# A retrieval layer's expert values: 160 instead of 128 tokens by gathered rows, 416-column matmuls, and a quarter of the value splits on GpSimd

## The reference, cut to what matters

```
eidx = ...        # per token: 8 heads x 16 experts out of 16384
gate = softmax(best_s)
u = u_tab[ib];  a = einsum('bd,bhkd->bhk', hb, u)
a = gelu(a) * gb
return einsum('bhk,bhkd->bd', a, v_tab[ib])     # 128 value rows of 2048 numbers per token
```

## Time and profile before

| | us |
|---|---|
| runs (three) | 5164.22, 5155.04, 5153.08; median 5155.04 |
| the profiled execution's own time | 5158.61 |
| its span, first to last instruction | 5157.0 |
| TensorE busy (x34141 matmuls) | 5036.2 (98%) |
| VectorE busy | 2321.4 (45%) |
| ScalarE busy | 1301.7 (25%) |
| GpSimd busy | 1060.5 (21%) |
| mean granted TensorE clock | 0.987 |

### The profile page before, as it was taken

The page is one execution under the profiler, slowest core; times in us unless marked ns, Lnnn a source line. Parts: engine busy times, 40 slices in busy tenths (PEclk is TensorE's granted clock), DMA queues, the critical chain, the costliest instruction groups (busy, mean ns, idle before and its releaser), DMA issues.

```text
span 5157.0 us, 86673 instructions
## 1 busy us (share of the span) xinstructions
PE 5036.2 (98%) x34141; PEld 4840.3 (94%) x34141; DVE 2321.4 (45%) x4396; ACT 1301.7 (25%) x1709; POOL 1060.5 (21%) x800
## 2 busy tenths in 40 slices
PE   8999999999998999999999999999999999999897
PEld 7999999999997999999999999999999999999797
DVE  4333442234326796122222200002788888888633
ACT  3113332133212112222222222222222222222232
POOL 1000000110000034333333344443212222212000
PEclk9999999899999999999999999999999999999998
DMA  5553345455543443345444443334777777777322
GB/s 171 156 159 114 122 154 161 135 161 169 168 122 97 147 139 104 106 159 179 159 163 163 159 157 104 104 133 166 262 258 255 274 261 258 266 260 249 106 74 77
DMA packets 503983, 855.15 MB, mean 166 GB/s; under 512 B 32496, under 2 KB 368384, under 8 KB 485008
## 3 DMA queue, kind: packets, MB, share of 16 engines
q1 hardware_dynamic: 188224, 472.44, 27.8%
q0 software_dynamic: 45296, 246.67, 12.7%
q10 hardware_dynamic: 270336, 134.25, 9.3%
HBM read 766.86 MB, written 222.56 MB: 192 GB/s over the span
## 4 chain that ended last, share of the span: by engine, by line
PE 95%; DVE 2%; issue 1%; ACT 0%; DMA 0%; DVEq 0%; ACTq 0%; POOL 0%; POOLq 0%
PE PS L1566 64%; PE PS L2016 24%; PE PS L1989 2%; PE PS L1590 1%; DVE h_lo L960 1%; PE PS L1680 0%; PE PS L1935 0%; PE PS L1618 0%; PE PS L1706 0%; PE PS L1823 0%; DVE rstd L936 0%; DVE hf L954 0%; PE PS L1813 0%; PE PS L1694 0%; ACT w_hi L589 0%
## 5 line engine op out<-in xcount | busy, mean ns | idle before, releaser
L1566 PE MATMUL PS<-h_hi,w_hi 128*128 128x288 f32 x7808 | 1715.0, 301 | 52.3 <-DVE h_lo L960 42.4
L1566 PE MATMUL PS<-h_hi,w_lo 128*128 128x288 f32 x7808 | 1680.1, 297 | 0.0
L1566 PE MATMUL PS<-h_lo,w_hi 128*128 128x288 f32 x7808 | 1678.3, 297 | 0.0
L1566 PEld LDWEIGHTS PS<-h_hi,w_hi 128*128 128x128 f32 x7808 | 1262.4, 190 | 93.5 <-issue 63.5
L1566 PEld LDWEIGHTS PS<-h_hi,w_lo 128*128 128x128 f32 x7808 | 1264.7, 190 | 0.0
L1566 PEld LDWEIGHTS PS<-h_lo,w_hi 128*128 128x128 f32 x7808 | 1264.4, 190 | 0.0
L589 ACT ACTIVATE w_hi<-w_raw 128x1024 fp32r<-128x1024 f32 x522 | 553.6, 1061 | 2307.3 <-PE PS L1566 2274.3
L519 POOL TENSOR_TENSOR w_lo<-w_raw,w_hi 128x1024 fp32r<-128x1024 f32 x254 | 618.9, 2437 | 1530.5 <-ACT w_hi L589 1530.5
L925 DVE TENSOR_TENSOR w_lo<-w_raw,w_hi 128x1024 fp32r<-128x1024 f32 x270 | 330.1, 1224 | 661.4 <-ACT w_hi L589 646.0
L1481 DVE TENSOR_TENSOR x<-x,PS 128x448 f32<-128x448 f32 x512 | 307.6, 618 | 229.0 <-PE PS L2016 220.9
L1418 DVE TENSOR_SCALAR oh_j<-iota,oh_cur 128x128 f32<-128x128 f32 x448 | 126.4, 282 | 585.0 <-PE PS L1989 584.9
(11 more groups left out here) (276 smaller groups left out, 4794.9 us busy)
## 6 DMA issues: line engine op xcount, KB each, us to landing
w_raw<-in_w SPq DMA_DIRECT2D x652, 512.0 KB, 4.1
v_rows<-in_w ACTq DMA_DIRECT2D x512, 256.0 KB, 3.7
v_raw<-in_w SPq DMA_DIRECT2D x128, 512.0 KB, 5.2
act_scr<-gsp POOLq DMA_DIRECT2D x128, 288.0 KB, 3.8
gate_scr<-g_st POOLq DMA_DIRECT2D x14, 2048.0 KB, 9.0
gl<-act_scr SPq DMA_DIRECT2D x32, 896.0 KB, 4.9
g_in<-gate_scr SPq DMA_DIRECT2D x32, 896.0 KB, 9.4
spill_scr<-spill POOLq DMA_DIRECT2D x40, 288.0 KB, 4.8
```

The source lines that it names most:

```text
L1566: ins = mm(dst[:, a], w[:, m, at + n], xx[:, k, a * TH:(a + 1) * TH], start=first and n == 0 and r == 0, stop=last and n == len(ks) - 1 an ...
```

## The change

- TG goes from 128 to 160 = P + TX tokens, TD from 448 to 416, ND from 14 to 13. The 32 extra tokens lie on four partitions each: partition 32q+t has experts 32q to 32q+31 of token 416+t. So each of the 32 groups now has GR_X = 5 rows, four for the 128 tokens and one (i = 4) for the extra ones, added to an accumulator of its own, `acc_x`; 160 rows, picks and `axpy` in all, five row buffers.
- `axpy` also runs in group 0 (at j = 3 to 7); in the others at j = 1, 2, 3, 6, 7, in the last at 0, 1, 2, 4, 5.
- The low part of the blocks with b % 4 == 2 is made on GpSimd (`value_low` there, semaphore `v_lop`), which has it in one order with `row` and `pick`; who waited for `v_lo` of such a block waits for `v_lop`.
- At the end 16 matmuls of 32 columns against `sel_x` sum the four partitions of each extra token; one more addition to x; TensorE waits for the additions before the next projection.
- The gate stage has 13 blocks of 32 tokens, the last outside the loop. Buffers are laid out anew.

```
-TG = 128
+TX = 32
+TG = P + TX
+GR_X = 5
+NK_G = GR_X * TX
...
+        def lowered(b):
+            q = b % 4
+            return ("v_lop", b // 4 + 1, 2) if q == 2 else ("v_lo", 3 * (b // 4) + min(q, 2) + 1, 6)
... (SyncE)
-                    sp.wait_ge(S["v_lo"], at_step(b - 3, bl))
+                    name, n, per = lowered(b - 4)
+                    sp.wait_ge(S[name], at_step(n, [(r, per * c) for r, c in loops]))
                     value_load(b, loops)
... (GpSimd)
+            def row(n):
+                if n >= GR_X:
+                    pool.wait_ge(S["axpy"], n - GR_X + 3)
+                pool.indirect_dma_start(rows[:, n % GR_X], None, v_rows, ...
+            def value_low(b):
+                pool.wait_ge(S["v_hi"], b + 1)
+                q = v_slot(b)
+                nc.gpsimd.tensor_tensor(q[2], q[0], q[1].bitcast(F32), ALU.subtract).then_inc(S["v_lop"], 1)
             pool.wait_ge(S["index"], 1)
             for u in range(2):
                 pool.wait_ge(S[f"asp{u}"], 16 * (PRE // 2))
             pool.wait_ge(s_used, B_PG)
+            pool.wait_ge(S["v_hi"], 3)
+            value_low(2)
             nc.gpsimd.memset(acc[:], 0.0).then_inc(S["axpy"], 1)
-            pick(0, 8)
+            nc.gpsimd.memset(acc_x[:], 0.0).then_inc(S["axpy"], 1)
+            for n in range(2 * GR_X):
+                pick(n)
             pool.wait_ge(S["relaid"], 32 * NV)
-            for k in range(P):
-                row(k)
-                if k % 8 >= 4 and k < P - 8:
-                    pick(8 * (k // 8 + 1) + 2 * (k % 4), 2)
+            for n in range(GR_X):
+                row(n)
+            for g in range(NG):
+                for i in range(GR_X):
+                    if g < NG - 1:
+                        row(GR_X * (g + 1) + i)
+                    if g < NG - 2:
+                        pick(GR_X * (g + 2) + i)
+                    if i == 1:
+                        value_low(8 * g + 6)
+                    if i == 3 and g < NG - 1:
+                        value_low(8 * g + 10)
... (VectorE, the indices)
-            ch.did(v.tensor_tensor(f_sel[:], iota[:], ident[:], ALU.mult))
+            quarters = [slice(TX * q, TX * q + TX) for q in range(4)]
+            src_x = slice(TD % P, TD % P + TX)
+            ch.did(v.tensor_tensor(f_one[:], iota[:], ident[:], ALU.mult))
+            ch.did(v.tensor_reduce(sel_x[:], ident[:].rearrange("p (e t) -> p t e", e=4), AX.X, ALU.add))
+            for r in quarters:
+                ch.did(v.tensor_copy(g_sel[r, :, 4], gij[src_x, TD // P, 0, r]))
...
+            for r in quarters:
+                ch.did(v.tensor_scalar(tok_x[r], part[r], float(TD - r.start), None, ALU.add))
+                ch.did(v.scalar_tensor_tensor(f_sel[r, :, 4], gij[src_x, TD // P, 1, r], float(NK),
+                                              gij[src_x, TD // P, 2, r], ALU.mult, ALU.add))
...
+            ch.did(v.tensor_scalar(f_sel[:, :, 4], f_sel[:, :, 4], float(T), tok_x[:], ALU.mult, ALU.add))
... (VectorE, the value stage)
+                turns = (0, 1, 2, 4, 5) if not more else (3, 4, 5, 6, 7) if g == 0 else (1, 2, 3, 6, 7)
                 if g:
                     dve.wait_ge(S["v_free"], at_step(KD * g, fl))
+                if turns[0] < 3:
+                    picked(g, loops)
                 for j in range(8):
...
-                    if more or j < 5:
+                    if (more or j < 5) and (j + 3) % 4 != 2:
                         value_low(8 * g + j + 3, loops)
...
+                    if j == 3 == turns[0]:
+                        picked(g, loops)
+                    if j in turns:
+                        axpy(g, turns.index(j), loops)
... (TensorE)
-            pe.wait_ge(S["axpy"], P + 1)
+            pe.wait_ge(S["axpy"], NK_G + 2)
...
+            for f in range(KD):
+                ins = mm(PS[:, 0, f * TX:(f + 1) * TX], acc_x[:, f * P:(f + 1) * P], sel_x[:], start=True, stop=True)
+            ins.then_inc(S["gx_t"], 1)
+            pe.wait_ge(S["gx"], 9)
```

More of the change, by code:

```diff
@@ L545, in _ @@
                     pool.dma_start(d["g_scr"][i * 2 + u], g_st[:, u]).then_inc(S[f"gput{u}"], 16)
+            for c in range(4):
+                put(UA + UG - 4 + c)
+            pool.wait_ge(S["g_ev"], 8 * ND + 2)
+            pool.dma_start(d["g_scr"][ND - 1], g_st[:, 0]).then_inc(S["gput0"], 16)
             puts(UA + UG, NCHUNK - 2 - UA - UG)
@@ L548, in _, with pick @@
             put(NCHUNK - 1, more=False)
[L551 to L564, removed]
+            def pick(n):
+                pool.indirect_dma_start(a_el[:, n:n + 1], None, act_flat,
+                                        bass.IndirectOffsetOnAxis(ap=act_i[:, n // GR_X, n % GR_X].unsqueeze(1), axis=0)
+                                        ).then_inc(S[f"el{n // GR_X % 2}"], 16)
+            def row(n):
+                if n >= GR_X:
+                    pool.wait_ge(S["axpy"], n - GR_X + 3)
+                pool.indirect_dma_start(rows[:, n % GR_X], None, v_rows,
+                                        bass.IndirectOffsetOnAxis(ap=row_i[:, n // GR_X, n % GR_X].unsqueeze(1), axis=0)
+                                        ).then_inc(S[f"row{n % GR_X}"], 16)
+            def value_low(b):
+                pool.wait_ge(S["v_hi"], b + 1)
+                q = v_slot(b)
+                nc.gpsimd.tensor_tensor(q[2], q[0], q[1].bitcast(F32), ALU.subtract).then_inc(S["v_lop"], 1)
             pool.wait_ge(S["index"], 1)
@@ L838, in _ @@
                         relay(i * 4 + (2 * s + c // 2), 6 + c % 2)
-            late = [(n, j) for n in range(4 * (ND // 2 - 1), N_FEAT) for j in (6, 7)]
+            for c in range(4):
+                beside(ND - 1, c)
+                relay(4 * (ND // 2 - 1) + c // 2, 6 + c % 2)
+            late = [(n, j) for n in range(4 * (ND // 2 - 1) + 2, N_FEAT) for j in (6, 7)]
             for c, (n, j) in enumerate(late):
@@ new lines, in axpy @@
+            def axpy(g, i, loops=()):
+                dve.wait_ge(S[f"row{i}"], at_step(16 * (g + 1), loops, 16))
+                n = GR_X * g + i
+                kl = [(r, GR_X * c) for r, c in loops]
+                dve.wait_ge(S["axpy"], at_step(n + 2, kl))
+                dst = acc if i < 4 else acc_x
+                v.scalar_tensor_tensor(dst[:], rows[:, i], a_sel[:, bass.ds(at_step(n, kl), 1)], dst[:], ALU.mult,
+                                       ALU.add).then_inc(S["axpy"], 1)
@@ L1487, in values @@
                         product(GRP * (g + 1) + (j + 1) // 2, loops)
-                    if k0 is not None and (j % 2 == 1 or not more):
-                        axpy(k0 + (j // 2 if more else j), [r for r, n in loops])
+                    if j == 3 == turns[0]:
+                        picked(g, loops)
+                    if j in turns:
+                        axpy(g, turns.index(j), loops)
             for c in range(GRP):
@@ L1493, in _ @@
                 low(c)
-            for b in range(3):
+            for b in range(2):
                 value_low(b)
@@ L1497, in _ @@
             with dve.Fori(0, (NG - 2) // 2) as i:
-                picked(0, [i])
                 for g in range(2):
-                    values(1 + g, [(i, 2)], k0=4 * g)
-            picked(P // 8 - 1)
-            values(NG - 1, more=False, k0=P - 8)
+                    values(1 + g, [(i, 2)])
+            values(NG - 1, more=False)
             dve.wait_ge(S["v_free"], 2 * NV)
```

103 lines of the change are left out of this document (56 added, 47 removed).

## The result

The changed kernel takes **5096.95 us** (median of four runs, 5095.67 to 5102.61); the kernel before, on the same chip, 5159.63 us (four runs, 5153.08 to 5165.33). The ratio is 0.9881 with a 95% interval of 0.9864 to 0.9898: faster by about 63 us. The forecast was 5087 us, between 5066 and 5120.

A forecast was written before the change was run, and what follows sets the result against it. The value stage was taken as bound by TensorE's matmul stream. Terms -85.2 - 6.6 + 2.1 + 18.5 + 2.0 + 1.4 = -67.8 took the profiled 5158.6 to 5090.8, median 5087 us, range 5066 to 5120.

The forecast's parts named there:

- The matmuls: Value stage: 416 columns instead of 448 take each matmul from 202.7 to 188.8 ns, 85 us less.
- rival of a pace set by weight loads: Value matmuls: weight loads, not columns, set the pace, so little is gained; about 5150 us, 2%.
- The gate stage: Gates: one block of 32 tokens fewer, 4 chunks x 16 small matmul instructions, 6.6 us less.
- The index block: Before the first one-hots: 14 more small VectorE instructions at 0.15 us, 2 us more, between 1 and 4.
- VectorE in a group: Value stage group: VectorE's work sums to 30.8 us against 36.25 on TensorE, so by itself it fits.
- the splits on GpSimd: Value groups: each shuts VectorE out up to 2.39 us, 4.8 a group: 35.6 of 36.25 us.
- hand-made plan: One value group laid out by instruction: GpSimd's split from 22.55 to 24.95 us, block 6 with 2.2 us to spare.
- No stall in a running group: Value groups: TensorE never waits, cost 0; bounds 0 to 2 us a group if a split comes late.
- rival of small stalls: Value groups: GpSimd misses the additions' gap; 0.5 to 2 us in 31 groups, 5102 to 5150 us, 14%.
- The start of the stage: Value stage, group 0: GpSimd's queue delays row 0 and block 6; TensorE stalls 18.5 us, plus 2 at low clock.
- The end: After the value matmuls: 16 extra small matmuls and one addition cost 1.4 us more, between 0.5 and 3.5.
- Slower: Value groups: `row`, `pick`, `axpy`, split form a ring making VectorE the bound; needs 2.2 us stall a group; 5%.

The follow-up runs named there:

- e6: Changed kernel with VectorE's index block spread over the eight steps of the last gate block instead of ahead of the first one-hots; 5092.00 us.
- e2: Changed kernel with GpSimd's order at the value stage's start altered: clearings, block 2's split, five picks, five rows, block 6's split, other picks; 5087.81 us.
- e5: e1 with GpSimd clearing its accumulators before waiting for the activations, then five picks, rows 0 to 4, then group 1's picks; 5074.27 us.
- e9: e5 and e6 together, with group 0's five `axpy` at j = 2, 3, 5, 6, 7 instead of 3 to 7; 5072.03 us.
- e10: e5 and e6 together, with the loads of blocks 4 and 5 issued ahead of the last activations' wait and group 2's loads; 5063.74 us.
- e4: Kernel before the change with only the quarter of the splits moved to GpSimd; 5177.92 us, ratio 1.0015 to 1.0056.
- e1: Changed kernel with all 256 splits on VectorE again; 5080.09 us.

## Why the prediction was right

- **The matmuls.** The step from two paces to a third held: 188.8 ns forecast, 188.89 measured. The rival of a pace set by weight loads is out.
- **The gate stage** held to the tenth: -6.6.
- **The index block** was a little undersized: 0.15 us an instruction gave 2.1, and 2.9 was measured. The four copies took 0.85 us together where 0.6 was put. The larger thing was not asked: the block stood on the path before the change too, and e6 takes it off for 7.6 us.
- **VectorE in a group, and the splits on GpSimd.** That a GpSimd split costs VectorE up to 2.39 us was right (2.0 and 2.2 here), and so was VectorE's busy time, 34.7 us against at most 35.6. The step that failed is "it fits": the sum put VectorE's waits at nothing, and it waits 1.8 us a group, mostly behind ScalarE, so that its round takes 36.53 us and not less than TensorE's 36.27. In group 1 the hand-made plan still holds, but for the pick that takes 3.07 us and not 1.51 beside an `axpy`: the split begins at 23.3 us instead of 22.55. Then it slips by 0.26 us a group to 24.8, the 2.2 us to spare are gone, and it falls on VectorE's split and not on additions. "No stall in a running group" became 0.24 to 0.28 us in 16 groups and 4.4 with its low clock once, 9.6 us in all with smaller waits in a few others. That is less than the cheapest price of the rival of small stalls (0.5 us in 31 groups), but it is the forecast's own sign of being wrong, TensorE waiting for the GpSimd split, in half of the groups if not in every one. The one late `row` has no cause that the trace shows; it stands in the same group 20 in e2 and e6 too (gaps of 2.7 us), so it is no accident of one execution.
- **The start of the stage.** 18.5 and 2.0 us were forecast, 16.7 and 1.8 measured, and the chain was the one laid out. Counted from the start of the stage, row 0 was issued at 25.6 us (forecast 25.2) and the first `axpy` over at 33.7 (33.6). One step was off: GpSimd's split got in between VectorE's `low` and `product` at 41.6 and did not have to wait until 44.1. (The forecast's own moments, 3619.8 less 3601, give 18.8 and not 18.5.) That the stall would go with the queue in front of row 0 was too simple; e5, e9 and e10 show a second limit behind it, VectorE's own work after a late block 4.
- **The end** cost nothing instead of 1.4 us: the 32 small matmuls took 3.7 us, as put, but the transposes ahead of them, no longer behind a wait of 2.98 us, took 1.94 instead of 3.23:

```profile
4760.38 1.94 PE L2100 MATMUL PS<-ident,acc 128*128 128x128 f32 x16 [0.77 <-DVE x L1546]
4762.15 3.72 PE L2104 MATMUL PS<-sel_x,acc_x 128*128 128x32 f32 x32
```

- **DMA** at 86% held, and is no limit in the groups.
- **Slower** did not come: it wanted 2.2 us of stall a group, and there are 0.3. Its mechanism is what the groups show, VectorE's round as the bound, at an eighth of that size; and e4 shows the splits on GpSimd alone, without the narrower matmuls, and there they do make the kernel slower.

So the gain is that of the columns and the gates, 91 us, of which 18.5 were given back at the start, 9.6 in the groups, 4 at the index block and ahead of it. The last 3.9 lie behind the projection and were luck for the most part: without them the two profiled executions would be 59 us apart, where the forecast had 67.8.

## What to carry to other kernels

Two engines that shut each other out are one resource: before work is moved from one to the other, add up both, with the full length of each GpSimd instruction on VectorE's account, and then the waits of the round behind a third engine, here 1.8 us of 36.5; a move that "fits" by busy time lost 15 to 20 us here, alone and within the change. And at the start of a stage look for loads and issues that are queued behind things needed only a group later: moving two loads ahead gave 5 to 7 us, and taking an index block off the path 7.6. Where one wait is taken away and the time stays, look at what was idle before it, for the second limit.

## What was not expected of the hardware

- GpSimd's own descriptor work is stretched by VectorE: picks took 1.73 us in the mean instead of 1.26, rows 1.26 instead of 0.95, and 1.8 to 3.0 us each where VectorE ran two-input instructions one after the other (e5, 3588 to 3611). The pick of 4011.70 ends at 4014.77, 0.83 us behind VectorE's `axpy`, and the one of 3993.10 0.86 us behind its own. With no GpSimd arithmetic (e1) rows are back at 0.96 and picks at 1.47.
- A one-input copy on GpSimd takes 1.05 us for 128x1024, less than half of the subtraction's 2.41, and shuts VectorE out only for that long.
- A matmul with its own weight load costs 188.9 ns at 416 columns, on the line between 133.3 at 288 and 202.7 at 448.
